# Two transformer blocks on one core: tile 1's normed output in one VectorE product with GpSimd's add, and the first norm weight as one row

## What is computed

```
h = rms_norm(x, norm_mix_pre)
x = x + rms_norm(hybrid_mixer(h, ...), norm_mix_post)
h = rms_norm(x, norm_ffn_pre)
x = x + rms_norm(swiglu(h, w_ffn_in, w_ffn_out), norm_ffn_post)

rms_norm(x, g) = x * rsqrt(mean(x * x) + EPS) * g      (fp32, over the 1024 features)
```

## Time and profile before

| | |
|---|---|
| median of three runs | 2284.57 us |
| profiled execution, its own time | 2285.04 us |
| its span, first to last instruction | 2283.0 us |
| TensorE busy | 2243.3 us, 98% |
| VectorE busy | 1426.3 us, 62% |
| ScalarE busy | 1108.6 us, 49% |
| GpSimd busy | 54.1 us, 2%, 46 instructions |
| mean granted TensorE clock | 0.997 of full |

### The profile page before, as it was taken

One profiled execution on the slowest core, in us unless ns is written; L12 is line 12 of the kernel. 1 busy time (PEld: TensorE's weight loads), 2 busy tenths in 40 slices (PEclk: granted clock), 3 DMA queues, 4 the chain that ended last, 5 costly groups with the idle time before them and its releaser, 6 DMA issues.

```text
span 2283.0 us, 38650 instructions
## 1 busy us (share of the span) xinstructions
PE 2243.3 (98%) x16940; PEld 2117.7 (93%) x16940; DVE 1426.3 (62%) x1563; ACT 1108.6 (49%) x1405; POOL 54.1 (2%) x46
## 2 busy tenths in 40 slices
PE   7999999999999999999999999999999999999998
PEld 7999998998899999899799999999889999999987
DVE  5778567445768757545587767455557775755554
ACT  4545645334554554434464535444446553444443
POOL 0000000000000000000000100000000010000000
PEclk9999999999999999999999999999999999999999
DMA  7545455555664554555545445455565444545653
GB/s 245 160 148 162 148 198 171 187 190 178 184 183 135 155 191 167 185 182 208 171 132 143 122 125 167 145 168 185 197 184 153 131 129 121 175 131 169 197 195 111
DMA packets 300956, 378.53 MB, mean 166 GB/s; under 512 B 26479, under 2 KB 260917, under 8 KB 300789
## 3 DMA queue, kind: packets, MB, share of 16 engines
q1 hardware_dynamic: 300788, 376.06, 52.4%
HBM read 369.67 MB, written 1.05 MB: 162 GB/s over the span
## 4 chain that ended last, share of the span: by engine, by line
PE 91%; DVE 5%; ACT 2%; issue 1%; DMA 0%; POOL 0%; SPq 0%; DVEq 0%; POOLq 0%; ACTq 0%
PE ps L590 26%; PE ps L2157 21%; PE ps L2699 7%; PE ps L959 5%; PE ps L2168 4%; PE ps L870 4%; PE ps L2227 4%; PE ps L647 2%; PE ps L605 2%; PE ps L2216 2%; PE ps L905 2%; PE ps L886 1%; PE ps L2429 1%; PE ps L755 1%; DVE a_wlo L1238 1%; DVE b_wlo L3032 1%
## 5 line engine op out<-in xcount | busy, mean ns | idle before, releaser
L590 PE MATMUL ps<-a_nhi,a_wlo 128*128 128x256 f32 x1664 | 475.2, 286 | 0.0
L590 PE MATMUL ps<-a_nlo,a_whi 128*128 128x256 f32 x1664 | 470.7, 283 | 0.0
L590 PE MATMUL ps<-a_nhi,a_whi 128*128 128x256 f32 x1664 | 470.6, 283 | 0.0
L1238 DVE TENSOR_TENSOR a_wlo<-a_ring,a_whi 128x2048 fp32r<-128x2048 f32 x173 | 393.5, 2286 | 112.6 <-ACT a_whi L985 112.1
L3032 DVE TENSOR_TENSOR b_wlo<-b_ring,b_whi 128x2048 fp32r<-128x2048 f32 (+1 forms) x168 | 379.4, 2261 | 129.1 <-ACT b_whi L2724 128.9
L985 ACT CAST a_whi<-a_ring 128x2048 fp32r<-128x2048 f32 x173 | 329.3, 1905 | 186.4 <-PE ps L590 59.7
L2724 ACT CAST b_whi<-b_ring 128x2048 fp32r<-128x2048 f32 (+1 forms) x168 | 316.4, 1884 | 125.8 <-PE ps L2699 79.0
L2157 PE MATMUL ps<-b_nhi,b_wlo 128*128 128x256 f32 x1232 | 355.4, 288 | 4.0 <-ACT b_gates L2779 3.1
L2157 PE MATMUL ps<-b_nhi,b_whi 128*128 128x256 f32 x1232 | 348.5, 283 | 0.0
L2157 PE MATMUL ps<-b_nlo,b_whi 128*128 128x256 f32 x1232 | 348.4, 283 | 0.0
L590 PEld LDWEIGHTS ps<-a_nhi,a_wlo 128*128 128x128 f32 x1664 | 319.0, 192 | 2.4 <-issue 1.7
(11 more groups left out here) (575 smaller groups left out, 4385.2 us busy)
## 6 DMA issues: line engine op xcount, KB each, us to landing
b_ring<-in_w_in SPq DMA_DIRECT2D x50, 1024.0 KB, 5.8
a_ring<-in_w_in SPq DMA_DIRECT2D x49, 1024.0 KB, 5.4
a_ring<-in_w_ffn_in SPq DMA_DIRECT2D x44, 1024.0 KB, 5.3
a_ring<-in_w_gate SPq DMA_DIRECT2D x32, 1024.0 KB, 5.4
b_ring<-in_w_up SPq DMA_DIRECT2D x32, 1024.0 KB, 5.5
b_ring<-in_w_down SPq DMA_DIRECT2D x32, 1024.0 KB, 4.9
a_ring<-in_w_ffn_out SPq DMA_DIRECT2D x22, 1024.0 KB, 5.0
a_ring<-in_w_branch SPq DMA_DIRECT2D x16, 1024.0 KB, 5.3
```

Source lines behind the costliest of these rows:

```text
L590: mm = T.matmul(out, w[:, k, c:c + P], x_[:, k, :], start=k == 0 and n == 0, stop=k == KD - 1 and n == 2)
L1238: nc.vector.tensor_tensor(part(wlo, h), part(ring, h), part(whi, h).bitcast(F32), ALU.subtract).then_inc(lo_ok, 1)
```

## The change

Two places of the first block are altered.

First, `norm_out` for tile 1. VectorE waits for the root first and makes PSUM output times root times gain in one instruction into `xm` (new L1311); a semaphore `gained` tells GpSimd, which adds `xm` to x in place, 128x1024, and signals `x_ok` (new L1679). Tile 0 is done as before. This happens at all four edges.

Second, the gain at the start of the first layer. It is loaded as one row of 4 KB into partition 0 (`gain_row`), issued second, and the identity third. TensorE multiplies the row by a row of 128 ones, in two products of 512 columns of plain fp32, into the PSUM banks 2 and 3 (new L853), and VectorE scales both tiles of layer 0 by the gain read from there. In the second layer the gain is loaded and read as before. The semaphore used for it is one that the end of the program uses as well, so two waits there are raised by one.

```diff
             if l == 0 and h == 0:
+                gain_row(sp_.engine)
+                start[0](sp_.engine)
                 sp_.dma_start(part(ring, 0)[:, 0:2, :], source(0)[:, 0:2, :]).then_inc(first_in, 16)
-                start[0](sp_.engine)
-                gain_in(sp_.engine, 0)
                 sp_.dma_start(part(ring, 0)[:, 2:4, :], source(0)[:, 2:4, :]).then_inc(landed[0], 16)
...
+    def gain_row(sp_):
+        sp_.dma_start(gpre1[0:1, :], a["norm_mix_pre"][0:1, :]).then_inc(gpost_in, 16)
...
-        dve.wait_ge(gpost_in, 16)
+        if l == 0:
+            dve.wait_for(first_gain, 1)
+        else:
+            dve.wait_ge(gpost_in, 16)
         dve.wait_ge(in_rs, t + 1)
-        scaled(0, t, gpre1)
+        scaled(0, t, gpre1 if l else first_gpre)
...
         if prior is None:
+            pe.wait_for(init_ok, 1)
+            pe.wait_ge(gpost_in, 16)
+            for j in range(2):
+                mm = T.matmul(ps[:, 2 + j, :], one_row, gpre1[0:1, 512 * j:512 * j + 512], start=True, stop=True)
+            mm.then_inc(first_gain, 1)
             turn_in(pe.engine, l, 0)
...
+            V.memset(one_row, 1.0)
             V.memset(asg[:, 8:16], -1.0).then_inc(init_ok, 1)
...
             dve.wait_ge(ssq_ok, n_ssq)
-            link(V.tensor_tensor(xm[:, t, :], ps[:, bank * t:bank * t + 2, :].rearrange("p a b -> p (a b)"),
-                                 gain[:, :], ALU.mult))
+            out = ps[:, bank * t:bank * t + 2, :].rearrange("p a b -> p (a b)")
+            if t == 1:
+                dve.wait_ge(rstd_ok, n_rstd)
+                V.scalar_tensor_tensor(xm[:, t, :], out, rstd[:, e, t:t + 1], gain[:, :], ALU.mult, ALU.mult
+                                       ).then_inc(gained, 1)
+                return
+            link(V.tensor_tensor(xm[:, t, :], out, gain[:, :], ALU.mult))
             dve.wait_ge(rstd_ok, n_rstd)
...
             root(e, t, 1)
+            if e != 3 and t == 1:
+                pool.wait_ge(gained, e // 2)
+                nc.gpsimd.tensor_tensor(x[:, t, :], x[:, t, :], xm[:, t, :], ALU.add).then_inc(x_ok, 1)
```

More of the change, by code:

```diff
@@ L149 @@
     "rope_ok": 10, "xs_ok": 1, "sc_ok": 2, "msq_ok": 1, "mx_ok": 12, "yt_ok": 1, "pn_ok": 12, "pt_v": 6,
-    "isc_ok": 1, "pen_ok": 2, "yl_ok": 4, "pr_free": 16, "mg_ok": 14, "ml_ok": 4, "x_ok": 4, "fu_free": 11,
-    "hs_ok": 11, "in_rs": 2, "rstd_ok": 7
+    "isc_ok": 1, "pen_ok": 2, "yl_ok": 4, "pr_free": 16, "mg_ok": 14, "ml_ok": 4, "x_ok": 4, "gained": 2,
+    "fu_free": 11, "hs_ok": 11, "in_rs": 2, "rstd_ok": 7
 }
@@ L343, in first_block @@
     in_ms, in_rs = sem("in_ms"), sem("in_rs")
-    first_in, first_hi, first_lo = sem("y_done"), sem("out_sq"), sem("out_ms")
+    first_in, first_hi, first_lo, first_gain = sem("y_done"), sem("out_sq"), sem("out_ms"), sem("out_rs")
+    one_row, first_gpre = y[0:1, 0, 0:P], ps[:, 2:4, :].rearrange("p a b -> p (a b)")
     ix_ps, ix_rl, isc_ok, pen_ok = (sem(n) for n in ("ix_ps", "ix_rl", "isc_ok", "pen_ok"))
@@ L351, in first_block @@
     fg_free, fu_free, hh_ok, hs_ok, dn_ps = (sem(n) for n in ("fg_free", "fu_free", "hh_ok", "hs_ok", "dn_ps"))
-    dch = sem("dch")
+    dch, gained = sem("dch"), sem("gained")
     def cols(src, l, c, n):
@@ L3598, in vector @@
             dve.wait_for(fin_in, 16)
-            dve.wait_for(out_rs, 1)
+            dve.wait_for(out_rs, 2)
             V.scalar_tensor_tensor(x[:, 0, :], x[:, 0, :], rstd[:, 0, 0:1], xm[:, 0, :], ALU.mult, ALU.mult
@@ L3613, in vector @@
                                    ).then_inc(out_ms, 1)
-            dve.wait_for(out_rs, 2)
+            dve.wait_for(out_rs, 3)
             for half in (slice(0, 512), slice(512, D)):
```

## The result

The changed kernel takes 2300.4 us, the median of six runs (2299.5 to 2301.01), against 2284.68 us for the kernel before (six runs): 15.7 us or 0.69% slower, ratio 1.0069 with a 95% interval of 1.0059 to 1.0079. The profiled execution has a span of 2298.6 us instead of 2283.0.

A forecast was written before the change was run, and what follows sets the result against it. TensorE, busy in 98% of the span, was taken to bound the kernel, so only its waits count. Edges +11.4, clock +2.9 and start -1.3 gave +13.0 us, forecast 2297.6 us, range 2288.5 to 2303.5.

The forecast's parts named there:

- at most one fall: First three edges (residual stream normalised for the next stage): TensorE's clock drops to 1.2 GHz at one at most; chance 0.52.
- three falls: Rival: TensorE's clock falls at two or three of the first three edges; 2303.4 us with three; chance 0.25.
- The add goes behind the split: At the first edge, GpSimd's add waits until VectorE's weight split, which has two SBUF inputs, ends at 384.25 us.
- The add's price: GpSimd's 128x1024 add at each edge: 2.4 us alone, between bounds of 0.95 and 2.85.
- The split 0.72 earlier, TensorE's wait shorter by as much: First edge: without the separate gain product, VectorE's weight split starts 0.72 us earlier and TensorE waits 0.72 less for it.
- The turn 2.9 late: First edge: TensorE transposes tile 1 2.9 us later because of the late add; charged alike at the first three edges.
- The last edge, +2.7: Edge into the second block: the split is 1.22 us long, the add ends at 1132.73 instead of 1130.07; +2.7 us.
- The clock: First three edges: TensorE's new idle time makes its clock fall at one of three, +2.9 us, with ends 0 and 8.7.
- The start, -1.3: Start of the first layer: scaling 0.9 us earlier and 0.4 less ScalarE delay, first product at 11.5 instead of 12.84; -1.3 us.
- An add that is first: Rival at the edges: GpSimd's add goes first and VectorE's split waits; +5.4 us in all, 2290.0; chance 0.06.
- An add beside the split: Rival at the edges: add and split run together; 2282.1 us with an add of 0.95; chance 0.07.
- a short add: Rival at the edges: the add runs at the memset's pace, 1.45 us less per edge, no fall; 2288.9 us; chance 0.10.

The follow-up runs named there:

- split_first: The changed kernel, but at each edge VectorE splits the weight part before the product of tile 1, so GpSimd's add meets no split; 2301.64 us.
- add_gets_in: The changed kernel with a small VectorE instruction (192 columns from PSUM) between product and weight split, so GpSimd's add starts first; 2297.73 us.
- clock_kept: The changed kernel with 26 products of no use on TensorE before the turn of tile 1 at the first three edges; 2296.12 us.
- row_filled: The kernel before with the new start (row's products before the identity wait) and 28 products of no use before the last edge's turn of tile 1; 2281.3 us.
- row_warm_filled: The kernel before with the new start, row's products before the identity wait, three products on zeros there, and 28 of no use at the last edge; 2281.78 us.
- add_on_vector: The changed kernel, but VectorE instead of GpSimd does the add of tile 1, between the product and the split; 2290.33 us.
- edges_only: The changed kernel with the old start: four edges changed, gain loaded as a broadcast again; 2301.09 us.
- start_only: The kernel before with the new start alone: gain loaded as one row and spread by TensorE, edges as before; 2283.33 us.
- half_add: The changed kernel with GpSimd adding only 512 of the 1024 columns, the other half left out; 2292.85 us (one run).
- row_first: The kernel before with the new start alone, TensorE making the row's two products before its wait for the identity; 2283.76 us.

## Why the prediction was right

The forecast was 2297.6 in a range of 2288.5 to 2303.5, slower with 0.88; measured were 2300.4. The way of the loss, an add held by the split and a late turn, was foreseen step by step. The clock was not: at most one fall had 0.52, and what happened, three falls, was a rival with 0.25. The steps:

- *The add goes behind the split.* Right, and shown from both sides by split_first and add_gets_in. The step that carried the case was to read the long roots as waits for VectorE's two-input instructions. The rule of the Trainium skill ("SBUF — State Buffer", section "Who interferes with whom"), by which the first to issue holds the ports for its whole instruction, agrees with the 4.35 and 2.37 us, and with 4.42 where the order was turned.
- *The add's price.* 2.4 taken, 2.37 measured. The bounds of 0.95 and 2.85 from the memset alone were wide, and the middle was luck as much as reasoning. The Trainium skill's figure ("GPSIMD Engine Reference", section "Elementwise — side-by-side cycle accounting"), halved to an estimate of 2.25, was 0.1 low.
- *The split 0.72 earlier, TensorE's wait shorter by as much.* Right: 1.37 became 0.72.
- *The turn 2.9 late.* Measured 2.95. By clock_kept an edge costs 3.3 even so. The difference is at the turn: TensorE now starts it when the first half is scaled and stands in it for the second (1.32 against 1.04 for the eight transposes in clock_kept), which it didn't before, having come 0.4 after the first half. That slack was seen, and its loss in the middle of the turn was not charged.
- *The last edge, +2.7.* The wait grew by 2.66, and the edge cost 2.6 up to VectorE's last instruction, 2.9 with the open 0.3 behind it.
- *The clock.* This term was wrong in both factors. One fall was charged out of three, at 2.9; there were three, at 1.3 to 1.6, because the low clock lasted half as long as at the last edge from which the price came: +4.4 where +2.9 stood. At the last edge itself, row_filled and row_warm_filled put the price at 2.0 to 2.3. As the idle time was nearest to the row that lost the clock, three falls was the likelier reading of the rows; but the rule behind both, that the length of the idle time decides, doesn't hold. The clock fell after 1.98 to 2.21 us in add_on_vector and not after 3.48 in edges_only. What else decides stays open. That the two errors, in the number of falls and in their price, went opposite ways kept the term within 1.5 us: that was luck.
- *The start, -1.3.* Scaling 0.6 to 0.9 earlier where 0.9 was expected, first product 0.9 to 1.2 earlier where 1.3 was; -1.24 in the medians of start_only. The -1.7 of the changed kernel's profile is more than that by the earlier rise of the clock, which the forecast didn't have. The products of the row took 3.78 us where 3.4 was priced.
- *The rivals.* An add that is first was measured as add_gets_in: 2297.7 where 2290.0 was worked out, since there too the clock falls, which that rival had left out: its +1.7 for an edge became 3.3 to 4.6. An add beside the split and a short add are ruled out. The rival of more falls is what happened in kind, at half its price.

From the forecast's parts: 11.4 + 2.9 - 1.3 = +13.0; from the measured ones: 4.6 + 5.0 + 4.8 + 2.9 - 1.7 = +15.6, of which 4.4 is the clock at three edges.

## What to carry to other kernels

Moving an elementwise step from VectorE to an idle GpSimd is not free of VectorE: ask which VectorE instruction runs right behind the hand-over and whether it has two SBUF inputs, for here the step took its own time plus nearly that instruction's: an add of 1.23 us on VectorE came to 4.35 on the path, and would have been 2.37 on GpSimd with nothing in its way. And a wait of about 2 us or more on TensorE has to be priced twice: once as a wait, once for the clock at which it may come back. At the first three edges of these profiles the clock fell with 15 of the 18 waits of 1.98 to 4.6 us and with none of those up to 1.65. Where the wait can't be removed, products of no use held the clock here (clock_kept, row_filled).

## What the runs showed of the hardware

- A GpSimd add of 128x1024 fp32 takes 2.34 to 2.37 us alone, of 128x512 1.1 less, and VectorE's of the same form 1.23. Whichever of it and VectorE's subtraction of two SBUF tiles (`wlo`, 2.28 us) is 0.1 to 0.2 us ahead runs at its own pace; the other takes nearly the sum, 4.35 or 4.42 us.
- TensorE stood 1.37 and 1.62 us and kept 2.4 GHz; after 1.99, 2.21 and 1.98 us (add_on_vector) its clock was at 1.2 GHz, within half a us of its first product. But it kept 2.4 GHz after 3.48 us in edges_only and after 2.60 and 2.37 us in half_add. A fall whose low clock lasted 3.4 us cost 1.3 to 1.6 us.
- TensorE at work from 1.8 to 8.5 us, first on zeros and then on operands of a single row, didn't bring the clock up sooner (16.3 us against 14.4 in row_first). Between kernels with the same start it rose at times from 15.1 to 17.7 us, which by the estimate above moves the result by about a microsecond.
